# Late projections in one piece ahead of the page stage, sample 4 in the ring's first slots

## The reference

```python
def _latent_attend(q_lat, q_pe, key_sets):
    for ckv, kpe, mask in key_sets:
        s = (einsum('bthc,bsc->bhts', q_lat, ckv) + einsum('bthr,bsr->bhts', q_pe, kpe)) * scale
        scores.append(s)
    probs = softmax(concatenate(scores, axis=-1), axis=-1)
    ... out = sum of einsum('bhts,bsc->bthc', probs_part, ckv)
```

## Time and profile before

| | |
|---|---|
| time, median of 3 runs | 1790.44 us (1788.96 to 1794.66) |
| the profiled execution | 1790.74 us, its span 1789.1 us |
| PE busy | 95% of the span |
| DVE, ACT, POOL busy | 32%, 22%, 7% |
| HBM read | 262.58 MB, 152 GB/s over the span |
| mean granted clock of PE | 0.987 |

### The profile page before, as it was taken

One profiled execution on the slowest core, in us unless ns is written; L12 is line 12 of the kernel. 1 busy time (PEld: TensorE's weight loads), 2 busy tenths in 40 slices (PEclk: granted clock), 3 DMA queues, 4 the chain that ended last, 5 costly groups with the idle time before them and its releaser, 6 DMA issues.

```text
span 1789.1 us, 27282 instructions
## 1 busy us (share of the span) xinstructions
PE 1707.5 (95%) x10992; PEld 1274.5 (71%) x10992; DVE 568.9 (32%) x1302; ACT 402.5 (22%) x899; POOL 125.5 (7%) x214
## 2 busy tenths in 40 slices
PE   7998899999999999999999988999999998999997
PEld 5676667677767777777766766776777676777775
DVE  1341564332023163330044324733220331533201
ACT  3231242131132231110132212412211332211101
POOL 1013000010010010000010030000000110000000
PEclk9999899999999999999999998999999999999999
DMA  9537222283337333343175272312734563333331
GB/s 351 173 117 260 107 97 73 71 320 119 142 148 300 144 124 127 133 146 118 51 264 181 82 260 108 119 49 85 305 125 156 191 272 108 118 141 137 127 118 50
DMA packets 64464, 273.54 MB, mean 153 GB/s; under 512 B 8529, under 2 KB 32530, under 8 KB 37074
## 3 DMA queue, kind: packets, MB, share of 16 engines
q1 hardware_dynamic: 51266, 208.57, 32.3%
q0 software_dynamic: 12512, 61.94, 9.2%
q10 hardware_dynamic: 560, 1.30, 0.2%
HBM read 262.58 MB, written 9.19 MB: 152 GB/s over the span
## 4 chain that ended last, share of the span: by engine, by line
PE 84%; DVE 6%; DMA 3%; issue 3%; ACT 2%; SPq 2%; POOL 0%; ACTq 0%; DVEq 0%; POOLq 0%
PE banks L813 42%; PE banks L842 15%; PE banks L764 6%; PE banks L797 5%; PE banks L820 5%; PE banks L871 4%; PE banks L761 3%; DVE work L1940 2%; DMA work<-in_ml_n 1%; PE banks L769 1%; SPq L604 1%; DVE o_branches L1940 1%; PE banks L1473 1%; PE banks L1492 1%; SPq L597 1%
## 5 line engine op out<-in xcount | busy, mean ns | idle before, releaser
L813 PE MATMUL banks<-h_normed,weight_ring 128*128 128x288 f32 x1888 | 459.4, 406 | 1.1 <-ACT h_normed L1557 1.1
L813 PEld LDWEIGHTS banks<-h_normed,weight_ring 128*128 128x128 f32 x1888 | 358.6, 190 | 100.5 <-ACT h_normed L1557 1.5
L842 PE MATMUL banks<-h_normed,weight_ring 128*128 128x288 f32 x1024 | 280.5, 417 | 7.1 <-ACT values_by_token L1723 4.6
L842 PEld LDWEIGHTS banks<-h_normed,weight_ring 128*128 128x128 f32 x1024 | 188.6, 191 | 64.0 <-issue 8.9
L813 PE MATMUL banks<-work,weight_ring 128*128 128x288 f32 (+1 forms) x960 | 226.8, 399 | 1.8 <-issue 1.8
L813 PEld LDWEIGHTS banks<-work,weight_ring 128*128 128x128 f32 x960 | 182.2, 190 | 46.1 <-issue 2.6
L1940 DVE TENSOR_TENSOR squares<-squares 128x288 f32<-128x288 f32 (+2 forms) x40 | 20.3, 508 | 329.4 <-ACT squares L1595 329.2
L797 PE MATMUL banks<-h_normed,weight_ring 128*128 128x288 f32 x448 | 116.6, 411 | 0.0
L1557 ACT ACTIVATE work<-banks 128x32 f32<-128x32 f32 (+8 forms) x142 | 55.9, 394 | 235.4 <-PE banks L764 62.0
L871 PE MATMUL banks<-h_normed,weight_ring 128*128 128x288 f32 x288 | 80.6, 437 | 21.3 <-DMA weight_ring<-in_w 14.2
L797 PEld LDWEIGHTS banks<-h_normed,weight_ring 128*128 128x128 f32 x448 | 82.4, 190 | 24.4 <-issue 4.3
(11 more groups left out here) (307 smaller groups left out, 1653.7 us busy)
## 6 DMA issues: line engine op xcount, KB each, us to landing
weight_ring<-in_w SPq DMA_DIRECT2D x171, 1024.0 KB, 4.8
work<-in_pool SPq DMA_DIRECT2D x112, 144.0 KB, 4.2
work<-in_mem_k POOLq DMA_DIRECT2D x12, 1024.0 KB, 11.1
work<-in_mem_v POOLq DMA_DIRECT2D x12, 1024.0 KB, 9.3
work<-in_pool POOLq DMA_DIRECT2D x64, 144.0 KB, 3.8
weight_ring<-in_pool SPq DMA_DIRECT2D x48, 144.0 KB, 3.0
projected<-in_mem_k POOLq DMA_DIRECT2D x4, 1024.0 KB, 24.5
projected<-in_mem_v POOLq DMA_DIRECT2D x4, 1024.0 KB, 6.0
```

Of the source, the lines that this page charges most:

```text
L813: last = mm(ps[:, bank, 0:width], block_of(first + k), rhs(k), start=k == 0, stop=k == n - 1)
L842: last = mm(ps[:, BANK[g], 0:N], block_of(t[2] + k), H[:, k, :] if t[0] == "gate" else O[:, 2 * n + k, :], start=k == 0, stop=k == t[3] - 1)
```

## The change

All 32 late blocks that lay inside the page stage are done in one piece ahead of its first scores. With them places 0 to 2 of the ring are free there, and sample 4 takes them in place of sample 7. Samples 5, 6 and 7 take the buffers of 0, of 1, and of 3 and 2. The waits of both issuing engines follow: sample 4 behind the last late projection, 5 behind `mla_pv` 1, 6 behind 2, slot 13 and sample 7 behind 4, slot 15 behind 6 (sample 5's values, and so 4's). PE does `scores(4)` inside pair 0. Mixing blocks are put elsewhere: 6 at once behind `scores(5)`, two behind `maxima(2)`, none between `scores(7)` and `maxima(3)`. Between the steps of pairs 0 and 1 there is nothing left but scores. One turn of maxima moves to bank 1, and ScalarE copies four late tiles ahead of `exps(0)`.

```diff
-        lent, o_half, first = groups(slots, 3 * SLOT * P, 3), groups(of, 4 * N, 1), groups(slots, 0, 4)
+        lent, o_half, first = groups(slots, 3 * SLOT * P, 3), groups(of, 4 * N, 1), groups(slots, 0, 5)
         kv = [whole[0:4], whole[4:8], lent + o_half, whole[8:11] + first[:1],
-              whole[0:4], whole[4:8], whole[8:11] + o_half, first]
+              first[1:5], whole[0:4], whole[4:8], whole[8:11] + o_half]
...
-        slot_after = {N_IN: 3, N_IN + 1: 3, N_IN + 2: 7}
+        slot_after = {N_IN: 3, N_IN + 1: 3, N_IN + 2: 5}
         S_BANK = (4, 5, 0, 1)
-        TOP_BANK = (2, 0, 2, 4)
+        TOP_BANK = (2, 1, 2, 4)
...
                     half = [page_numbers(sp, b, (0, 1)) for b in range(4, NB)]
+                    sp.wait_ge(*at("gemm_done", slot_done(N_IN - 1)))
+                    cache(sp, layer, 4, half[0])
                     sp.wait_ge(*at("mla_pv", 1))
-                    cache(sp, layer, 4, half[0])
+                    cache(sp, layer, 5, half[1])
                     sp.wait_ge(*at("mla_pv", 2))
-                    cache(sp, layer, 5, half[1])
+                    cache(sp, layer, 6, half[2])
                     for s in range(N_IN, NSLOT):
                         if s in slot_after:
                             sp.wait_ge(*at("mla_pv", slot_after[s] + 1))
                         slot(s)
                         if s == N_IN:
                             sp.wait_ge(*at("mla_pv", 4))
-                            cache(sp, layer, 6, half[2])
-                            sp.wait_ge(*at("gemm_done", slot_done(N_IN - 1)))
                             cache(sp, layer, 7, half[3])
...
+                    fill(32)
                     scores(0)
                     scores(1)
-                    fill(4)
+                    scores(2)
                     maxima(0)
-                    scores(2)
+                    scores(3)
                     maxima_back(0)
-                    scores(3)
                     shares(0)
-                    fill(4)
+                    scores(4)
                     maxima(1)
                     values(0)
                     maxima_back(1)
-                    fill(4)
                     outputs(0)
-                    fill(2)
                     shares(1)
-                    fill(4)
                     values(1)
-                    fill(4)
                     outputs(1)
-                    fill(6)
-                    scores(4)
-                    fill(4)
                     scores(5)
-                    mix(3)
+                    mix(6)
                     maxima(2)
-                    mix(5)
+                    mix(8)
                     maxima_back(2)
-                    mix(6)
                     scores(6)
                     shares(2)
                     scores(7)
-                    mix(8)
                     maxima(3)
                     values(2)
                     maxima_back(3)
-                    mix(9)
+                    mix(10)
                     outputs(2)
                     mix(12)
                     shares(3)
```

More of the change, by code:

```diff
@@ L699, in _ @@
                     cache(pool, layer, 3, third, "kv_full_pool")
+                    pool.wait_ge(*at("gemm_done", slot_done(N_IN - 1)))
+                    cache(pool, layer, 4, half[0], "kv_full_pool")
                     pool.wait_ge(*at("mla_pv", 1))
-                    cache(pool, layer, 4, half[0], "kv_full_pool")
+                    cache(pool, layer, 5, half[1], "kv_full_pool")
                     pool.wait_ge(*at("mla_pv", 2))
-                    cache(pool, layer, 5, half[1], "kv_full_pool")
+                    cache(pool, layer, 6, half[2], "kv_full_pool")
                     pool.wait_ge(*at("mla_pv", 4))
-                    cache(pool, layer, 6, half[2], "kv_full_pool")
-                    pool.wait_ge(*at("gemm_done", slot_done(N_IN - 1)))
                     cache(pool, layer, 7, half[3], "kv_full_pool")
@@ L1696, in _ @@
                     step(A(l_rows[0:4, :], l_rows[0:4, :], ACT.Exp), "ml_exp")
+                    for i in range(4):
+                        late_out()
                     exps(0)
-                    late_out()
                     exps(1)
-                    for i in range(3):
-                        late_out()
                     exps(2)
```

## The result

The changed kernel took 1811.41 us (median, 1809.1 to 1817.41), beside 1789.97 us for the kernel before: a ratio of 1.012 [1.0089, 1.015], 21.4 us slower. The profiled execution took 1810.43 us with a span of 1808.8, 19.7 longer than the 1789.1 before.

The account below looks back on a forecast made before the run. PE, busy 95%, bounds the kernel, with gaps where the page stage's second half runs at the DMA rate. Layer 0 +5.6 and layer 1 +7.1 on 1790.7 give 1803.4 us; range 1793 to 1813.

Parts of the forecast that it names:

- the give-back: mLSTM stage: DVE's wait for the mLSTM state goes, with most of PE's 3.29; 4.5 us gained in layer 0, 4.2 in layer 1.
- The late run: Ahead of the first scores: 32 late blocks in one piece of 15.6 us, from 128.69 to 144.3.
- SyncE's page numbers: Page stage: SyncE reads 32 numbers from 129.8 to 147.1, one reason given for the DMA engines' empty stretch, 134 to 144.
- Sample 4: Page stage: its data lands at 154.3, scores(4) due from 154.2; no wait there, or under 1 us.
- Slot 13: Mixing's first block: read 19.9 us after sample 5's first page, at 178.7, with PE idle 8.0 us before it.
- The steps of pairs 0 and 1: Page stage without cover: sample 0 done at 158.4, sample 3 at 167.4, scores(5) ending at 170.65.
- Behind the slot: From slot 13's reader at 178.7 to maxima(3) at 188.25, plus 2.1 us for PE's lower clock.
- Early clock: Pairs 0 and 1: six idle pieces of 0.3 to 2 us cost 0 to 4 us in clock; 0.5 taken.
- Rival (c): Clock stays down over pairs 0 and 1: 3.5 and 0.7 us more a layer, 1811.8 us; chance 0.15.
- Rival (a): Slot 13 lands at its bound and the gain behind is whole: 5.7 us less a layer, 1792; chance 0.13.
- (b): Faster: slot 13 lands before scores(5) end, PE doesn't stand at mix(6), 1783.2 us; chance 0.07.
- (d): Sample 4 late for scores(4): pages landing 3 us later shift all of pair 0, +6 in all, 1809.4; chance 0.05.

Follow-up runs that it names:

- the kernel with the same program up to this reader: Against the changed kernel, slot 15 (with 16 and 17 behind it) waits for mla_pv 8 again, as in the kernel before: 1816.74 us, ratio 1.0145.
- the cut kernel: Changed kernel with only the first 128 of 288 words of each page row of samples 4 to 7 transferred: 1797.15 us, ratio 1.0035.
- the reordered kernel: Changed kernel with maxima(2), scores(6) and maxima_back(2) put ahead of mix(6), slot 13's reader: 1801.63 us, ratio 1.0053.
- the clock held up: Changed kernel with 25 unread matmuls a layer in the page stage's gaps, 12 of them ahead of mix(6): 1809.61 us, ratio 1.0099.
- The cut pair: Kernel before and changed kernel, both with 128 of 288 words per row transferred for samples 4 to 7: 1784.52 and 1797.15 us.

## Why the prediction was right, and where it was off

Forecast 1803.4, range 1793 to 1813, slower with 0.78; measured 1811.4. The direction, the place of the long wait (PE behind slot 13) and the give-back were right. The size was +12.7 against +21.4 in the medians and +19.7 between the profiled executions. Four of the signs I had named were missed: scores(4) waited 1.29 and 1.08 us where I allowed 1, the slot's wait was 4.3 and 4.5 where I had 6 to 8, and in layer 0 DVE's wait became 0.9 where I had it gone and PE's 3.29 became 1.17 where I had under 1. The terms, from the start of each stage:

| term | predicted | layer 0 | layer 1 |
|---|---|---|---|
| start to SyncE's first page of sample 5 | 30.1, and 0.5 for the clock | 32.56 | 30.82 |
| from there to slot 13's first reader | 19.9 | 21.48 | 19.54 |
| from there to maxima(3), clock included | 9.55 + 2.1 | 11.58 | 12.22 |
| give-back to the end of the mLSTM stage | -4.7, -4.4 | -3.96 | -3.9 |

- **The late run, SyncE at sample 4**: 15.7 us in one piece, and the first page at 146.18, behind 32 numbers. As predicted.
- **SyncE's page numbers, read with too much in them.** I gave them as one reason for the empty stretch from 134 to 144. They can't be: the buffer for sample 4 was free only at 143.4, and GpSimd's first page of it went out at 143.97. The numbers cost SyncE the 4.1 us from 143.4 to 147.53.
- **Sample 4, off.** I had its scores wait 0, at most 1. They waited 1.29 and 1.08, and in layer 0 they ran at half clock. That is the 2.45 that sample 5's first page came late there, since it waits for sample 0's values behind these scores. In layer 1, where these scores ran at the full clock, it is 0.7.
- **Slot 13, the other term that was short in layer 0.** I took 19.9 from the earlier trace rows. Layer 1 gave 19.54, layer 0 21.48. SyncE issued the slot 11.5 us behind sample 5's first page in both layers, so the difference of 1.9 comes behind the issue: 9.95 us to the reader against 8.04. Why it does is open; the DMA engines were full in both (some 400 GB/s). With the 2.45 above it makes +4.0; less the 0.5 that I took for the early clock this is 3.5, the whole of layer 0's miss. That layer 1 came out within 0.4 is in part luck, for the kernel with the same program up to this reader took 4.5 us more there.
- **The steps of pairs 0 and 1, the worst term of the sum.** From the stage's start to the end of scores(5) I summed 42.0 us. It was 49.7 in layer 0 and 45.8 in layer 1, with 47.5 in layer 0 of the cut kernel, in which nothing behind hides it. The miss didn't show in the time because PE then stands at a slot whose time it sets only in part: 8.0 us idle predicted, 4.30 and 4.52 measured. The places of the wait and of its releaser were right. That so large a miss cost nothing here is how the kernel is built, and not a merit of the sum.
- **Behind the slot**: 11.65 predicted, 11.58 and 12.22 measured. The 2.1 of clock is in it: the twelve matmuls of mixing take 4.84 and 5.48 us, against 3.15 in layer 1 of the reordered kernel.
- **Early clock, mis-sized.** I took 0.5 a layer. Rival (c) had 4.2 a layer more, clock and knock-on together, and its time, 1811.8, is nearly the one measured. Its clock came true in layer 0:

```profile
154.20:157.40 3.20, 3.04 (x36) 1.81 (x40) 0.85 (x2) 0.00 (x0) 0.00 (x0) 0.50 0.00 0
157.60:164.00 6.40, 4.59 (x90) 3.46 (x83) 1.68 (x7) 1.19 (x4) 3.35 (x7) 1.00 0.46 130
164.40:184.60 20.20, 13.70 (x123) 9.14 (x124) 2.85 (x8) 0.00 (x0) 9.13 (x18) 0.50 1.05 389
```

20 us at 1.2 GHz. It was entered behind idle pieces of 0.9 to 1.6 us, for which I had put the price low; the slot's 4.30 lies inside it. In layer 1 the same pieces cost less (0.50 from 1058.7 to 1065.3, and again around the slot). But (c) isn't the cause of the whole miss either: with the clock held up, the slot was read as late as before and only 1.8 us came back. It came within 0.4 us of the time, for a reason of which the runs show the clock and not the cost. The Trainium skill (TensorE: Matmul & The Clock Gate, HAM oscillation) tells of PE that waits on DMA between short groups of matmuls; the trace agrees that the clock falls, and shows that waits for ScalarE and VectorE of about a microsecond do it too.
- **Give-back, right**: 4.7 and 4.4 predicted (with the 0.2), 3.96 and 3.9 measured. Its mechanism is shown from both sides, by holding the slots back (+5.3) and by freeing the state in the kernel before (-9.1). What I named as next late came: DVE's own chain, with 2.57 in place of 1.21.
- **Outside the two stages** I had 0; it was +1.9.
- **Rival (a), (b), (d)**: the bound put the slot's reader at 46.7 to 48.2 us behind the stage's start. With whole pages it never came before 50.4. Where PE was ready sooner, the slot was not: 13.4 us from issue to reader instead of 9.95. Nor was there time for (b): even with the pages cut, the changed kernel is slower. As (d) feared, sample 4 was late, by 1.3 and 1.1 us and not 3.

The sum: layer 0 missed by 3.5 to maxima(3), layer 1 by 0.4, the give-back by 0.7 and 0.5, the rest of the program by 1.9; 7.0 in all, which is 19.7 - 12.7.

**What the cover was worth** I never priced as such. I summed the steps one after the other and found the slot later than their end, so their gaps looked free. The kernel with nothing but the fills moved shows the price of that move as it stands, 28 us, later transfers included. The cut pair shows that some 12 of the change's 21.4 stay when these pages' bytes are more than halved. The other 9 are near the 9.8 that the reordered kernel won, which too takes PE from behind the slot. Whether they are the same microseconds no run tells, since the two edits were not made together.

## What to carry to other kernels

Work without a deadline that stands between latency-bound steps is their cover: before you move it out to have data sooner, move it alone and look, for here that alone cost 28 us, some of it through transfers that then started later, and the new buffers and the new order gave back some 3. Put the reader of a late transfer behind all that is already resident (9.8 us here for five lines of order). And take a gain by the least edit that gives it: one wait on SyncE brought 9 us, of which the large change got some 8 as well and lost them again.

## What the runs showed of the hardware

- **Half clock through small gaps.** In layer 0 the granted clock fell to 1.2 GHz at 164.3, when no idle piece of the stage had been longer than 1.64 us (0.89 the last), and stayed there for 20 us, the slot's wait included. In the same steps of layer 1, with the same pieces, it was 6.6 us before the slot. Which layer is hit early does not hang on the program alone: in three kernels whose programs are the same up to there, the first eight matmuls of scores(4) took 1.93 or 1.94 us in layer 0 of the changed one, in layer 1 of the reordered one and in both of the one with the slots held back, and 1.06 or 1.07 us in the other two places. Matmuls that nobody reads held the clock at 1.00 from 150 to 179.5. Yet they won 1.8 us in one kernel, and the other lost 5, for the most part unexplained: a higher clock ahead of a wait is spent in the wait (4.99 us of it, where it was 4.30).
- **An issuing engine that is the late one.** Each page number costs SyncE a load of 270 ns with 147 and 18 ns behind it, 0.54 us from one to the next; 32 of them hold it for 17.4 us. For most of these sample 4's buffer was not yet free; the last 4.1 were late. Reading half of the numbers earlier made the kernel before 6.5 us faster, of which 1.9 are seen in the page stages. The Trainium skill (DMA: Bandwidth & Descriptors, Issuing engines are not separate DMA queues) says that the sequencer's time to start a DMA is usually small beside the DMA itself. Here it was not: the issue of a page took 0.58 us and its number 0.54, and by estimate its 144 KB take 0.4 us at the 370 GB/s of the earlier trace rows.
- **A slot issued sooner, read no sooner.** Issued at 171.42 it was read 9.95 us later, issued at 169.04 13.4 us later; in layer 1 it was 8.0 and 11.9. Both times the DMA engines moved some 400 GB/s from 168 to 178. GpSimd's pages of sample 7 started some 3 us sooner in the second case; that they took what the slot lost is likely, and was not tried by itself.
